# Token transposes ahead of the modulation with its columns tile by tile, and the last eight expert picks one by one, in a two-block transformer kernel on one core

## The chip, the core and the metric

The kernel is one program on one of the eight cores of a Trainium2 chip. TensorE (PE) multiplies matrices from SBUF into the eight banks of PSUM, VectorE (DVE) and ScalarE (ACT) do elementwise work, GpSimd (POOL) issues the indexed gathers, and SyncE's queue (SPq) issues the other transfers, which sixteen DMA engines carry out. The metric is the device time of one execution in microseconds (us).

## The reference

256 tokens of width 1024 pass two transformer blocks, all in float32. What the change touches is the first step of the first block and the last step of the second:

```python
# first block, the first step (c is one row of 1024; w_ada is 1024 x 6144)
mod = silu(c) @ w_ada + b_ada
shift1, scale1, gate1, shift2, scale2, gate2 = split(mod, 6)
hmix = rmsnorm(x, norm_mix_w) * (1.0 + scale1) + shift1
proj = hmix @ w_in                       # 1024 x 3600, all mixers' inputs
...
# second block, the last step (PEER): every token has 8 heads x 16 picks = 128 experts of 16384
act = gelu(einsum(u_tab[expert], x))     # one dot product of 1024 for each token and pick
w = gate * act
x = x + einsum(w, v_tab[expert])         # one row of 1024 for each token and pick
```

Between the two lie convolutions, a gated delta rule, window attention, a mixture of 32 experts, gated linear attention and block attention.

## The kernel before

Everything is written by engine: each of the five engines has its own list of instructions, and semaphores order them. Tokens are in two tiles of 128 (`t`), features in eight chunks of 128 (`k`).

**The head of the kernel.** The first block's matmuls are a hand-written list of jobs (`head_jobs`). A job has a name, a PSUM bank and the engine that empties it ("D" for DVE, "A" for ACT). TensorE fills the banks in that order and counts each job in the semaphore `hd`; before it writes a bank it waits until the last job of that bank has been emptied (`hbank`). DVE and ACT count what they empty in `ev_d` and `ev_a`. A job that is added by `add` takes the next bank of eight in turn.

SyncE loads c, x, the identity and ones, then four tiles of `w_ada` of 2 MB each (columns 0 to 2047: shift1 and scale1), a small tail of `w_in` (`in_tail`, 16 columns), and the first tiles of `w_in`, each 2 MB; the order is one queue.

DVE computes the root mean square of each token and writes the scaled tokens `h_tok` (L1927). TensorE multiplies the condition with each of the four tiles (`condition`, L1128): 8 matmuls with 512 columns, each of which the trace shows as two instructions, as for every float32 matmul here. DVE copies each result to `part1` (L1932). After the fourth copy the job `col` turns shift1 and scale1 into one column per chunk, by 16 matmuls with one column (L1140), and DVE makes `mod_t` of them (L1935 to L1938) and posts `mod1_ready`. TensorE has by then gone on to transpose the tokens (`xT0` to `xT3`, 16 transposes of 128 x 128, L1149). DVE (L1944) and ACT (L780) empty these four banks, and apply scale and shift of a chunk as they copy it from PSUM to `hT`, two chunks a bank, eight instructions with 256 columns in all. Then come the job `gab` (16 columns of `w_in`, L1120), and the projections `k0`, `k1`, `q0`, `q1`, `v0`, `v1` (L1114), each two chunks of 128 output features.

**The end of the kernel.** PEER's 256 picks (128 for each token tile) are gathered one by one: a pick brings one row of 2048 numbers for each of 128 tokens, u and v side by side, 1 MB. For pick `i` DVE takes the dot product (`dot`, L2726). In batches of `BATCH = 4`, ACT takes the GELU of four dot products (`applied`, L1056), DVE multiplies them by the gates (`weights`, L2734), and ACT makes four diagonal matrices of the products (L1063), in four buffers: diagonal `i` waits for `v_free` at `i - 3`. TensorE multiplies each diagonal with the v row in two halves (`values`, L1712) and accumulates in two banks over 128 picks. DVE issues its instructions in this order:

```python
for i in range(16 * N_STEP):
    if i >= 4:
        dot(i)
    if i >= 2 * BATCH and i % BATCH == 1:
        weights(i // BATCH - 1)
    ...
weights(16 * N_STEP // BATCH - 1)
result(1)
```

So the weights of picks 244 to 247 follow dot 249, those of 248 to 251 follow dot 253, and the last four follow dot 255. `result` adds the two finished banks to x (L2741) after the last pick, and SyncE writes each half out.

Of the kernel before, what the change touches and what calls it, by code (L numbers as in the profile page):

```python
# [15 lines left out]
ALU = mybir.AluOpType  # L16
ACT = mybir.ActivationFunctionType
# [98 lines left out]
def head_jobs():  # L116


    jobs = [("ada0", 0, "D"), ("ada1", 1, "D"), ("ada2", 0, "D"), ("ada3", 1, "D"), ("col", 2, "D"),
            ("xT0", 4, "D"), ("xT1", 5, "D"), ("xT2", 6, "A"), ("xT3", 7, "A"), ("gab", 3, "D")]  # L120
# [6 lines left out]
    for name in ("k0", "k1", "q0", "q1", "v0", "v1", "ss"):  # L127
        add(name, "D")
# [58 lines left out]
HEAD_OPS = {"col": 2, "xT0": 2, "xT1": 2, "xT2": 2, "xT3": 2, "k0": 4, "k1": 4, "q0": 4, "q1": 4, "v0": 4, "v1": 4,  # L187
# [117 lines left out]
UV_PLACES = 16  # L305
UV_PLAN = uv_plan(16 * TT * PH)
# [25 lines left out]
def two_blocks(nc, io):  # L332
    ctx = ExitStack()
    with ctx:
# [231 lines left out]
        h_ready = sem("h_ready")  # L566
        conv_scaled = sem("conv_scaled")
# [72 lines left out]
        diag_ready = sem("diag_ready")  # L640
        p_taken = sem("p_taken")
# [101 lines left out]
        def _(act):  # L743
# [30 lines left out]

            act.wait_ge(mod1_ready, 1)
            for g in (2, 3):
                b = halves(done(f"xT{g}"))
                for c in range(2):
                    k = 2 * g + c
                    act.activation(hT[:, k, :], b[:, c, :], ACT.Identity, scale=mod_t[:, 8 + k:9 + k],  # L780
                                   bias=mod_t[:, k:k + 1]).then_inc(ev_a, 1)
# [297 lines left out]
        def _(pe):  # L1079
# [52 lines left out]
            pe.wait_ge(cond_ready, 1)  # L1132
            for n in range(N_ADA1):
                b = hbank(f"ada{n}")
                hfull(condition(b, head_tile("ada", n)))
            b = hbank("col")
# [568 lines left out]
            def values(first, last_):  # L1705
                for i in range(first, last_):
# [144 lines left out]
        def _(dve):  # L1851
# [77 lines left out]

            for i in range(N_ADA1):  # L1930
# [17 lines left out]
            b = hjob("gab")  # L1948
            took(dve.tensor_copy(gab, b[:, 0:32].rearrange("p (a b) -> p a b", a=2)))
            hsync()  # L1950
            t3 = lambda ap: ap.rearrange("p (t c) -> p t c", t=TT)
            o(dve.tensor_tensor(t3(g_t), gab[:, :, 0:8], bc(dt_b.unsqueeze(1), [P, TT, 8]), ALU.add))
            post(gab_in)
# [18 lines left out]
            side_taps("k1", 6)  # L1972
            side_taps("q0", 0)
# [756 lines left out]
            def weights(b):  # L2730
                s, k = b * BATCH // 16, b * BATCH % 16
                sync()
                dve.wait_ge(gelu_done, b + 1)
                dve.tensor_tensor(w_cur[:, s, k:k + BATCH], gel[:, s, k:k + BATCH],  # L2734
                                  gates[:, s // 2, s % 2, k:k + BATCH], ALU.mult).then_inc(w_ready, 1)
# [41 lines left out]
            weights(16 * N_STEP // BATCH - 1)  # L2777
# [62 lines left out]
```

## Time and profile before

| | |
|---|---|
| median of three runs | 1695.36 us (1693.72 to 1697.14) |
| profiled execution, its own time | 1694.07 us |
| its span, first to last instruction | 1692.2 us |
| TensorE busy | 1475.6 us, 87% |
| VectorE busy | 784.0 us, 46% |
| ScalarE busy | 265.1 us, 16% |
| mean granted TensorE clock | 0.949 of full speed |
| data moved | 551.06 MB, mean 326 GB/s |

The span runs from the first to the last instruction; the execution's own time is 1.87 us more. Times in the rows are counted from the start of the span. The granted clock has two levels, shown as 1.00 (2.4 GHz) and 0.50 (1.2 GHz); a stretch that holds both shows a value between. The ends of matmuls are modelled, so the distance between starts is the safer measure of a matmul's price.

### The profile page before, as it was taken

The page shows a single profiled execution, that of the slowest core. Times are in us where ns is not written, and L with a number is a line of the kernel's source. Part 1 is how long each engine was busy: PE and PEld are TensorE (multiplying, and loading weights), DVE is VectorE, ACT ScalarE, POOL GpSimd, SP SyncE. Part 2 cuts the span into 40 slices and gives each one's busy share as a digit, 9 for nine tenths or more (in the row PEclk, how much of TensorE's full clock was granted, in tenths as well). Part 3 has the DMA queues.
Part 4 walks back from the last instruction along what each step waited for, and adds up shares of the span by engine and source line. Part 5 has one row for each costly group of instructions (what it writes and reads, how often), then busy time and mean ns, then how long its engine had stood idle before and what let it go on. Part 6 is the DMA issues. An engine that isn't in the chain of part 4 may idle for free.

```text
span 1692.2 us, 16785 instructions
## 1 busy us (share of the span) xinstructions
PE 1475.6 (87%) x6282; PEld 800.6 (47%) x6282; DVE 784.0 (46%) x1830; ACT 265.1 (16%) x644; POOL 308.1 (18%) x288
## 2 busy tenths in 40 slices
PE   4999999599999999999699798898777777787877
PEld 2897885444444444443446575553333333333333
DVE  2116754513232322322333466376766666676553
ACT  1312221100000000000033321222212121212111
POOL 0001000100000000000000012355444444444440
PEclk8999999699999999999899899999999999889999
DMA  9532347389999999999405138799999999999994
GB/s 376 226 108 96 147 150 298 130 344 427 428 428 427 426 423 427 427 429 428 203 33 216 51 137 304 305 376 422 421 422 421 421 422 421 422 421 421 421 422 200
DMA packets 60273, 551.06 MB, mean 326 GB/s; under 512 B 8608, under 2 KB 8896, under 8 KB 10400
## 3 DMA queue, kind: packets, MB, share of 16 engines
q1 hardware_dynamic: 22192, 277.47, 39.7%
q0 software_dynamic: 38000, 272.50, 39.4%
q8 instruction: 52, 0.85, 0.2%
q14 instruction: 29, 0.24, 0.0%
HBM read 548.90 MB, written 1.05 MB: 325 GB/s over the span
## 4 chain that ended last, share of the span: by engine, by line
PE 47%; DMA 39%; issue 5%; DVE 5%; POOL 2%; ACT 2%; SPq 0%; DVEq 0%; POOLq 0%; ACTq 0%
DMA ring<-peer_uv_d,work 19%; DMA ring<-expert_w_d 14%; PE ps L1462 9%; PE ps L1120 7%; PE ps L1712 7%; DMA consts_sb<-peer_uv_d,work 5%; PE ps L1212 5%; PE ps L1114 5%; PE ps L1571 4%; PE ps L1502 2%; PE ps L1451 1%; PE ps L1369 1%; DMA ring<-w_ada_d 1%; POOL ring L1845 1%; PE ps L1473 1%
## 5 line engine op out<-in xcount | busy, mean ns | idle before, releaser
L1712 PE MATMUL ps<-ring,work 128*128 128x512 f32 x752 | 364.6, 637 | 92.5 <-ACT work L1063 92.5
L2726 DVE CUSTOM_DVE_ANT_0 ring<-ring,work 128x1024 f32<-128x1024 f32 x188 | 229.8, 1223 | 134.8 <-DMA ring<-peer_uv_d,work 133.1
L1712 PEld LDWEIGHTS ps<-ring,work 128*128 128x128 f32 x752 | 149.3, 204 | 301.9 <-issue 178.9
L1845 POOL DMA_INDIRECT ring<-peer_uv_d,work x188 | 205.7, 1094 | 269.1 <-PE ps L1712 180.1
L1462 PE MATMUL ps<-ring,work 128*64 128x512 f32 x1024 | 226.6, 597 | 9.3 <-DMA ring<-expert_w_d 8.5
L1462 PEld LDWEIGHTS ps<-ring,work 128*64 128x64 f32 x1024 | 77.9, 138 | 154.8 <-issue 153.6
L1120 PE MATMUL ps<-ring,hT 128*128 128x512 f32 (+1 forms) x288 | 123.0, 586 | 1.7 <-issue 0.8
L1063 ACT ACTIVATE work<-consts_sb,work 128x128 f32<-128x128 f32 x256 | 82.3, 390 | 266.4 <-DVE work L2734 263.2
L1502 PE MATMUL ps<-ring,work 128*64 128x512 f32 x512 | 113.4, 595 | 0.7 <-DVE work L2356 0.7
L1712 PE MATMUL ps<-work 128*128 128x512 f32 x136 | 78.0, 703 | 39.9 <-ACT work L1063 39.9
L2352 DVE TENSOR_TENSOR work<-work,ps 128x512 f32<-128x512 f32 x16 | 11.0, 688 | 199.1 <-PE ps L1462 199.1
L1820 POOL DMA_DIRECT2D mod<-subkeys_d x1 | 0.5, 547 | 488.6 <-DVEq L2411 488.6
L1120 PEld LDWEIGHTS ps<-ring,hT 128*128 128x128 f32 x288 | 55.6, 196 | 63.1 <-issue 61.1
L1114 PE MATMUL ps<-hT,ring 128*128 128x256 f32 x352 | 79.6, 389 | 0.0
L922 ACT ACTIVATE work<-ps 128x512 f32<-128x512 f32 x16 | 9.6, 597 | 442.1 <-PE ps L1462 442.1
L1571 PE MATMUL ps<-hT,ring 128*128 128x128 f32 x640 | 73.8, 276 | 0.0
L1571 PEld LDWEIGHTS ps<-hT,ring 128*128 128x128 f32 x640 | 72.9, 193 | 1.5 <-issue 1.4
L1114 PEld LDWEIGHTS ps<-hT,ring 128*128 128x128 f32 x352 | 68.4, 196 | 9.6
L1212 PEld LDWEIGHTS ps<-ring 128*128 128x128 f32 x608 | 69.2, 192 | 5.2 <-issue 4.2
L1212 PE MATMUL ps<-ring 128*128 128x128 f32 x608 | 69.6, 275 | 0.8 <-ACT ring L853 0.8
L1451 PEld LDWEIGHTS ps<-work 128*128 128x128 f32 x512 | 60.0, 196 | 15.9 <-issue 12.2
L1502 PEld LDWEIGHTS ps<-ring,work 128*64 128x64 f32 x512 | 35.3, 137 | 67.4 <-issue 66.5
(388 smaller groups left out, 1502.3 us busy)
## 6 DMA issues: line engine op xcount, KB each, us to landing
ring<-expert_w_d SPq DMA_DIRECT2D x96, 2048.0 KB, 15.7
ring<-w_in_d SPq DMA_DIRECT2D x13, 2048.0 KB, 18.0
ring<-w_ada_d SPq DMA_DIRECT2D x12, 2048.0 KB, 8.1
ring<-w_out_d SPq DMA_DIRECT2D x4, 2048.0 KB, 8.0
ring<-peer_w_query_d SPq DMA_DIRECT2D x4, 2048.0 KB, 7.7
ring<-peer_uv_d,work POOLq DMA_INDIRECT x188, 23.4
mod<-b_ada_d SPq DMA_DIRECT2D x1, 2048.0 KB, 26.8
consts_sb<-consts_d SPq DMA_DIRECT2D x1, 1346.0 KB, 26.4
```

What stands on the lines that cost most here:

```text
L1063: act.activation(diag[:, k % 4, :], ident, ACT.Copy, scale=w_cur[:, s, k:k + 1]).then_inc(diag_ready, 1)
L1114: last = pe.matmul(b[0:n, at:at + T], wt[:, k, c0:c0 + n], hT[:, k, :], start=(k == 0), stop=(k == KC - 1))
L1120: last = pe.matmul(b[:, at:at + n], hT[:, k, t * P:(t + 1) * P], wt[:, k, c0:c0 + n], start=(k == 0), stop=(k == KC - 1))
L1212: last = pe.matmul(b[:, h * P:(h + 1) * P], lhsT(h), rhs(h), start=True, stop=True)
L1369: last = pe.matmul(ps[MID.bank(f"w{t}{n}")][:, :], mixT[k][:, t * P:(t + 1) * P], slot(N_HEAD - 2 + n)[:, k, :], start=(k == 0), stop=(k = ...
L1451: last = pe.matmul(b[:, c * P:(c + 1) * P], h_tok[:, t, k * P:(k + 1) * P], pm[:, t, :], start=(t == 0), stop=(t == TT - 1))
L1462: last = pe.matmul(b[u * CAP:(u + 1) * CAP, :], xeT[:, k, u * CAP:(u + 1) * CAP], wt[u][:, k, :], start=(k == 0), stop=(k == KC - 1), skip ...
L1502: last = pe.matmul(b[u * CAP:(u + 1) * CAP, :], actT[:, c, u * CAP:(u + 1) * CAP], wt[u][:, c, n * 512:(n + 1) * 512], start=(c == 0), sto ...
L1571: last = pe.matmul(b[0:n, at:at + P], wt[:, k, c0:c0 + n], hT[:, k, t * P:(t + 1) * P], start=(k == 0), stop=(k == KC - 1))
L1712: last = pe.matmul(ps[V_BANK[t] + n][:, :], diag[:, i % 4, :], v_row(i)[:, n * 512:(n + 1) * 512], start=(i % (16 * PH) == 0), stop=(i % ( ...
L1845: pool.indirect_dma_start(out=uv_rows(i), out_offset=None, in_=io["peer_uv"], in_offset=bass.IndirectOffsetOnAxis(ap=idx[:, s, k:k + 1], a ...
L2726: dve.tensor_tensor_reduce(out=u_row(i), in0=u_row(i), in1=h_tok[:, i // (16 * PH), :], scale=1.0, scalar=0.0, op0=ALU.mult, op1=ALU.add, ...
```

## The change

The four transposes' jobs move to the front of TensorE's list, before the first `w_ada` tile, and are emptied by plain copies (DVE two banks, ACT two banks). The columns of a `w_ada` tile are made right behind the matmuls of the next tile, so that only the fourth tile's columns (4 matmuls) are left when its copy is done. Eight matmuls of the identity with itself, whose result nothing reads (`warm`), follow each of the first three tiles. Scale and shift are then applied in place in `hT`: DVE takes chunks 0 to 4 and ACT chunks 5 to 7. The job `gab` moves behind `k1`, with its emptying on DVE behind that of `k1`, and takes a bank of the round, which moves the later jobs' banks by one. At the end, the last eight picks each get their own GELU, weights and diagonal; the weights of picks 244 to 247 follow dot 248 instead of dot 249; and the first half of the last result waits for the first half of the last pick alone (`half_done`).

```diff
-    jobs = [("ada0", 0, "D"), ("ada1", 1, "D"), ("ada2", 0, "D"), ("ada3", 1, "D"), ("col", 2, "D"),
-            ("xT0", 4, "D"), ("xT1", 5, "D"), ("xT2", 6, "A"), ("xT3", 7, "A"), ("gab", 3, "D")]
+    jobs = [("xT0", 4, "D"), ("xT1", 5, "D"), ("xT2", 6, "A"), ("xT3", 7, "A"), ("ada0", 0, "D"), ("ada1", 1, "D"),
+            ("ada2", 0, "D"), ("ada3", 1, "D"), ("col", 2, "D")]
...
-    for name in ("k0", "k1", "q0", "q1", "v0", "v1", "ss"):
+    for name in ("k0", "k1", "gab", "q0", "q1", "v0", "v1", "ss"):
...
+def batches(n):
+    return [(i, BATCH) for i in range(0, n - 8, BATCH)] + [(i, 1) for i in range(n - 8, n)]
+PICKS = batches(16 * TT * PH)
...
@@ ScalarE, head
+            for g in (2, 3):
+                act.activation(hT[:, 2 * g:2 * g + 2, :], halves(done(f"xT{g}")), ACT.Copy).then_inc(ev_a, 1)
             act.wait_ge(mod1_ready, 1)
-            for g in (2, 3):
-                b = halves(done(f"xT{g}"))
-                for c in range(2):
-                    k = 2 * g + c
-                    act.activation(hT[:, k, :], b[:, c, :], ACT.Identity, scale=mod_t[:, 8 + k:9 + k],
-                                   bias=mod_t[:, k:k + 1]).then_inc(ev_a, 1)
+            act.wait_ge(ev_a, head_evacuated("xT3"))
+            for k in (5, 6, 7):
+                act.activation(hT[:, k, :], hT[:, k, :], ACT.Identity, scale=mod_t[:, 8 + k:9 + k],
+                               bias=mod_t[:, k:k + 1]).then_inc(hx_a, 1)
@@ ScalarE, picks
-                for i in range(first, last, BATCH):
+                for b, (i, size) in enumerate(PICKS):
+                    if not first <= i < last:
+                        continue
                     s, k0 = i // 16, i % 16
-                    act.wait_ge(dotted, i + BATCH)
-                    act.activation(gel[:, s, k0:k0 + BATCH], dots[:, s, k0:k0 + BATCH], ACT.Gelu).then_inc(gelu_done, 1)
+                    act.wait_ge(dotted, i + size)
+                    act.activation(gel[:, s, k0:k0 + size], dots[:, s, k0:k0 + size], ACT.Gelu).then_inc(gelu_done, 1)
...
-                    act.wait_ge(w_ready, i // BATCH + 1)
-                    for k in range(k0, k0 + BATCH):
+                    act.wait_ge(w_ready, b + 1)
+                    for k in range(k0, k0 + size):
@@ TensorE, head
+            def warm(n):
+                for _ in range(n):
+                    pe.matmul(ps[3][:, 0:P], ident, ident, start=True, stop=True)
             pe.wait_ge(in_first, 16)
-            evacuated("ada3")
-            for c in range(4 * N_ADA1):
-                last = pe.matmul(b[:, c:c + 1], part1[:, c // 4, c % 4 * P:(c % 4 + 1) * P], ones[:, 0:1],
-                                 start=True, stop=True)
-            hfull(last)
             pe.wait_ge(h_ready, 1)
             for g in range(4):
                 b = hbank(f"xT{g}")
...
-            b = hbank("gab")
-            pe.wait_ge(in_tail, 16)
-            evacuated("xT1")
-            evacuated("xT3")
-            token_major(b, 0, 0, tail_w, 0, 16)
-            hfull(token_major(b, 16, 1, tail_w, 0, 16))
+            def columns(n):
+                b = ps[HEAD[HEAD_AT["col"]][1]]
+                evacuated(f"ada{n}")
+                for c in range(4 * n, 4 * n + 4):
+                    last = pe.matmul(b[:, c:c + 1], part1[:, n, c % 4 * P:(c % 4 + 1) * P], ones[:, 0:1],
+                                     start=True, stop=True)
+                return last
+            pe.wait_ge(cond_ready, 1)
+            for n in range(N_ADA1):
+                b = hbank(f"ada{n}")
+                hfull(condition(b, head_tile("ada", n)))
+                if n:
+                    columns(n - 1)
+                if n < N_ADA1 - 1:
+                    warm(8)
+            hbank("col")
+            hfull(columns(N_ADA1 - 1))
+            pe.wait_ge(hx_d, 5)
+            pe.wait_ge(hx_a, 3)
...
+                if name == "k":
+                    gate_columns()
@@ TensorE, picks
+                        if n == 0 and i == 16 * N_STEP - 1:
+                            last.then_inc(half_done, 1)
@@ VectorE, head
+            for g in range(2):
+                b = halves(hjob(f"xT{g}"))
+                took(dve.tensor_copy(hT[:, 2 * g:2 * g + 2, :], b))
             for i in range(N_ADA1):
...
-            for g in range(2):
-                b = halves(hjob(f"xT{g}"))
-                for c in range(2):
-                    k = 2 * g + c
-                    took(dve.tensor_scalar(hT[:, k, :], b[:, c, :], mod_t[:, 8 + k:9 + k], mod_t[:, k:k + 1],
-                                           ALU.mult, ALU.add))
+            dve.wait_ge(ev_a, head_evacuated("xT2"))
+            for k in range(5):
+                dve.tensor_scalar(hT[:, k, :], hT[:, k, :], mod_t[:, 8 + k:9 + k], mod_t[:, k:k + 1],
+                                  ALU.mult, ALU.add).then_inc(hx_d, 1)
...
             side_taps("k1", 6)
+            gates_in()
             side_taps("q0", 0)
@@ VectorE, picks
             def result(t):
                 for n2 in range(2):
-                    dve.wait_ge(v_free, 16 * PH * (t + 1))
+                    if t and n2 == 0:
+                        dve.wait_ge(half_done, 1)
+                    else:
+                        dve.wait_ge(v_free, 16 * PH * (t + 1))
...
-                if i >= 2 * BATCH and i % BATCH == 1:
+                if i >= 2 * BATCH and i % BATCH == 1 and i < 16 * N_STEP - 8:
                     weights(i // BATCH - 1)
+                if i == 16 * N_STEP - 8:
+                    weights((16 * N_STEP - 8) // BATCH - 1)
+                if i >= 16 * N_STEP - 8:
+                    weights((16 * N_STEP - 8) // BATCH + i - (16 * N_STEP - 8))
...
-            weights(16 * N_STEP // BATCH - 1)
             result(1)
```

## Rows read from the trace of the kernel before

**Rows 1.** The page's chain that ended last, shares of the span by engine.
```profile
PE 47%; DMA 39%; issue 5%; DVE 5%; POOL 2%; ACT 2%; SPq 0%; DVEq 0%; POOLq 0%; ACTq 0%
```

**Rows 2.** The chain in order of time, 0 to 110 us: start, us, what.
```profile
4.91 23.78 DMA ring<-w_ada_d
...
28.82 1.96 PE ps L1128 x16
...
30.80 0.70 DVE work L1932
...
31.64 4.88 PE ps L1140 x32
...
39.29 1.94 ACT hT L780 x4
...
41.36 4.43 PE ps L1120 x32
45.80 44.16 PE ps L1114 x192
```

**Rows 3.** Timeline, 0 to 45 us: start, us, engine, line, shapes, idle before.
```profile
6.16 19.21 SPq L687 DMA_DIRECT2D ring<-w_in_d x2
...
9.39 1.41 DVE L1927 TENSOR_SCALAR work<-x,small 128x1024 f32<-128x1024 f32 x2
...
13.85 3.39 PE L1128 MATMUL ps<-ring,work 128*32 128x512 f32 x16 [13.85 <-DMA ring<-w_ada_d]
...
23.64 3.62 PE L1128 MATMUL ps<-ring,work 128*32 128x512 f32 x16 [3.06 <-DMA ring<-w_ada_d]
...
36.38 3.65 PE L1149 MATMUL ps<-consts_sb,work 128*128 128x128 f32 x16
36.63 0.17 DVE L1935 TENSOR_TENSOR small<-ps,small 128x8 f32<-128x8 f32 x1 [5.14 <-PE ps L1140]
...
37.52 1.90 DVE L1944 TENSOR_SCALAR hT<-ps,small 128x256 f32<-128x256 f32 x4 [0.36 <-PE ps L1149]
```

**Rows 4.** Stretches of 2 us: busy time by engine (count), granted clock, DMA.
```profile
32.00:34.00 2.00, 2.00 (x19) 2.00 (x20) 0.00 (x0) 0.00 (x0) 0.00 (x0) 0.98 1.00 426
34.00:36.00 2.00, 2.00 (x12) 2.00 (x11) 0.00 (x0) 0.00 (x0) 0.00 (x0) 0.50 1.01 426
...
42.00:44.00 2.00, 2.00 (x20) 2.00 (x19) 0.00 (x0) 0.00 (x0) 0.00 (x0) 1.00 1.02 434
...
48.00:50.00 2.00, 2.00 (x6) 1.59 (x5) 0.00 (x0) 0.00 (x0) 0.00 (x0) 0.50 0.93 396
```

**Rows 5.** DMA issues from 6 to 15 us: KB, us to landing.
```profile
ring<-w_in_d SPq DMA_DIRECT2D x1, 2048.0 KB, 27.8
```

**Rows 6.** Groups by form, 30 to 250 us: busy us, mean ns.
```profile
L2048 DVE TENSOR_SCALAR work<-work,small 128x256 f32<-128x256 f32 x2 | 0.6, 342 | 0.0
```

**Rows 7.** Timeline of the end, from 1623 us.
```profile
1623.83 1.88 PE L1712 MATMUL ps<-consts_sb,work 128*128 128x512 f32 x4
1625.55 1.88 PE L1712 MATMUL ps<-work 128*128 128x512 f32 x4
...
1654.56 6.09 PE L1712 MATMUL ps<-ring,work 128*128 128x512 f32 x13
...
1658.48 1.23 DVE L2726 CUSTOM_DVE_ANT_0 ring<-ring,work 128x1024 f32<-128x1024 f32 x1 [1.26 <-DMA ring<-peer_uv_d,work]
...
1672.21 1.28 ACT L1063 ACTIVATE work<-consts_sb,work 128x128 f32<-128x128 f32 x4 [4.79 <-DVE work L2734]
...
1672.66 13.79 PE L1712 MATMUL ps<-ring,work 128*128 128x512 f32 x28 [2.77 <-ACT work L1063]
...
1675.80 1.23 DVE L2726 CUSTOM_DVE_ANT_0 mod<-mod,work 128x1024 f32<-128x1024 f32 x1 [1.23 <-DMA mod<-peer_uv_d,work]
...
1677.07 0.20 ACT L1056 ACTIVATE work<-work 128x4 f32<-128x4 f32 x1 [3.58 <-DVE work L2726]
...
1688.21 1.52 DVE L2741 TENSOR_TENSOR x<-x,ps 128x512 f32<-128x512 f32 x2 [10.67 <-PE ps L1712]
```

More of the change, by code:

```diff
@@ L184 @@
 HEAD_AT = {name: i for i, (name, _, _) in enumerate(HEAD)}
-HEAD_OPS = {"col": 2, "xT0": 2, "xT1": 2, "xT2": 2, "xT3": 2, "k0": 4, "k1": 4, "q0": 4, "q1": 4, "v0": 4, "v1": 4,
+HEAD_OPS = {"col": 2, "k0": 4, "k1": 4, "q0": 4, "q1": 4, "v0": 4, "v1": 4,
             "gc": 3, "kq0": 2, "kq1": 2, "kk0": 2, "kk1": 2}
@@ L566, in two_blocks @@
         h_ready = sem("h_ready")
+        hx_d = sem("hx_d")
+        hx_a = sem("hx_a")
         conv_scaled = sem("conv_scaled")
@@ L640, in two_blocks @@
         diag_ready = sem("diag_ready")
+        half_done = sem("half_done")
         p_taken = sem("p_taken")
@@ L1130, in condition @@
                 return last
[L1132 to L1136, printed above, removed]
-            pe.wait_ge(in_first, 16)
-            evacuated("ada3")
-            for c in range(4 * N_ADA1):
-                last = pe.matmul(b[:, c:c + 1], part1[:, c // 4, c % 4 * P:(c % 4 + 1) * P], ones[:, 0:1],
-                                 start=True, stop=True)
-            hfull(last)
+            def warm(n):
+                for _ in range(n):
+                    pe.matmul(ps[3][:, 0:P], ident, ident, start=True, stop=True)
+            pe.wait_ge(in_first, 16)
             pe.wait_ge(h_ready, 1)
@@ L1151, in _, with gate_columns @@
                 hfull(last)
-            b = hbank("gab")
-            pe.wait_ge(in_tail, 16)
-            evacuated("xT1")
-            evacuated("xT3")
-            token_major(b, 0, 0, tail_w, 0, 16)
-            hfull(token_major(b, 16, 1, tail_w, 0, 16))
+            def columns(n):
[17 more added lines that the diff above has]
+            pe.wait_ge(hx_a, 3)
+            def gate_columns():
+                b = hbank("gab")
+                pe.wait_ge(in_tail, 16)
+                token_major(b, 0, 0, tail_w, 0, 16)
+                hfull(token_major(b, 16, 1, tail_w, 0, 16))
             def two_chunks(name, wt, c0):
@@ L1939, in _, with gates_in @@
             post(mod1_ready)
-            for g in range(2):
-                b = halves(hjob(f"xT{g}"))
-                for c in range(2):
-                    k = 2 * g + c
-                    took(dve.tensor_scalar(hT[:, k, :], b[:, c, :], mod_t[:, 8 + k:9 + k], mod_t[:, k:k + 1],
-                                           ALU.mult, ALU.add))
-            dve.wait_ge(in_small, 80)
-            b = hjob("gab")
-            took(dve.tensor_copy(gab, b[:, 0:32].rearrange("p (a b) -> p a b", a=2)))
-            hsync()
+            dve.wait_ge(ev_a, head_evacuated("xT2"))
+            for k in range(5):
+                dve.tensor_scalar(hT[:, k, :], hT[:, k, :], mod_t[:, 8 + k:9 + k], mod_t[:, k:k + 1],
+                                  ALU.mult, ALU.add).then_inc(hx_d, 1)
+            dve.wait_ge(in_small, 80)
+            def gates_in():
+                b = hjob("gab")
+                took(dve.tensor_copy(gab, b[:, 0:32].rearrange("p (a b) -> p a b", a=2)))
+                hsync()
+                o(dve.tensor_tensor(t3(g_t), gab[:, :, 0:8], bc(dt_b.unsqueeze(1), [P, TT, 8]), ALU.add))
+                post(gab_in)
             t3 = lambda ap: ap.rearrange("p (t c) -> p t c", t=TT)
-            o(dve.tensor_tensor(t3(g_t), gab[:, :, 0:8], bc(dt_b.unsqueeze(1), [P, TT, 8]), ALU.add))
-            post(gab_in)
             scaled = [0]
@@ L2730, in weights @@
             def weights(b):
-                s, k = b * BATCH // 16, b * BATCH % 16
+                i, size = PICKS[b]
+                s, k = i // 16, i % 16
                 sync()
                 dve.wait_ge(gelu_done, b + 1)
-                dve.tensor_tensor(w_cur[:, s, k:k + BATCH], gel[:, s, k:k + BATCH],
-                                  gates[:, s // 2, s % 2, k:k + BATCH], ALU.mult).then_inc(w_ready, 1)
+                dve.tensor_tensor(w_cur[:, s, k:k + size], gel[:, s, k:k + size],
+                                  gates[:, s // 2, s % 2, k:k + size], ALU.mult).then_inc(w_ready, 1)
             def result(t):
                 for n2 in range(2):
-                    dve.wait_ge(v_free, 16 * PH * (t + 1))
+                    if t and n2 == 0:
+                        dve.wait_ge(half_done, 1)
+                    else:
+                        dve.wait_ge(v_free, 16 * PH * (t + 1))
                     xs = x[:, t, n2 * 512:(n2 + 1) * 512]
```

## The prediction

> **What bounds the kernel now.** I read the chain that ended last first, as shares: TensorE and DMA hold 86% of it between them [rows 1], so a gain exists only where the change shortens what one of these two waits for. Then the same chain in order of time over the head [rows 2]. The reader is to see three stretches there. Up to 28.7 us the chain is the loading of the four `w_ada` tiles. From 28.8 to 45.8 us it is a relay, with no transfer in it: fourth tile's matmuls, its copy, 32 column instructions (L1140), transposes, scale and shift (ACT, L780), `gab` (L1120). From 45.80 us it is 44.16 us of unbroken projections, to 89.96 us. The relay is what the head's part of the change attacks. The timeline [rows 3] says what TensorE does before: it works 3.39 us on the first tile at 13.85 us and then waits for tiles, while the scaled tokens, which the transposes need, are finished at 9.39 + 1.41 = 10.80 us.
>
> The stretches of 2 us [rows 4] show the granted clock. TensorE is busy all the time from 31.64 us, yet the level falls from 1.00 to 0.50 at 34 us, and it is at 0.50 again at 48 to 50 us, in `k0`. So the relay is partly run at 1.2 GHz: 19 one-column instructions in 2 us at the high level, 12 at the low one.
>
> For the end I read the timeline [rows 7]. Dot 248 starts at 1658.48 and dot 255 at 1675.80 us: 17.32 / 7 = 2.47 us from dot to dot, each released by its gather. TensorE needs less for a pick: 1625.55 - 1623.83 = 1.72 us for four matmul instructions. It idles between batches, and at the end the idle time turns against it: the diagonals of picks 248 to 251 are made only at 1672.21 us, behind dot 253, and from 1672.66 us TensorE has eight picks before it, until the result's add starts at 1688.21 us, 11.1 us after the last dot. The eight picks take 15.5 us instead of 8 x 1.72 + 0.2 = 13.9: the first of them run at the lower level, after 2.77 us of idling.
>
> **The head, step by step.** Removed from the relay: the transposes, 28 - 4 = 24 of 32 column instructions (12 of 16 matmuls), and `gab`, which is not saved but moved between `k1` and `q0`.
>
> *Transposes first.* They can start at about 10.9 us and cost 3.65 us as in [rows 3], at the low level, so they end at 14.6 us. The first tile's matmuls start at 14.6 instead of 13.85 us. Its cover: the second tile is the next event and lands some 4.9 us after the first (23.78 us of loading hold four tiles and 1 MB of x before them [rows 2]). The plain copies (two by DVE, two by ACT) fall in time in which both engines wait. They cost nothing; without that cover a DVE copy of a bank costs 0.70 us [rows 2].
>
> *Per tile.* At the high level: 1.96 us for the tile [rows 2], 8 x 0.105 = 0.84 us for the earlier tile's columns (19 in 2 us [rows 4]), and the eight extra matmuls, 16 instructions at 3.65 / 16 / 2 = 0.114 us, so 1.83 us. The sum is 4.6 us, under the 4.9 us between tiles, with 0.3 us to spare: nothing at the high level. At the low level: 3.62 + 8 x 0.167 + 3.65 = 8.6 us, and TensorE would fall behind the transfers. I take the high level, because the engine would be busy over 90% of the time from 11 us on, where before it had gaps of 3 us ahead of the tiles that ran low [rows 3].
>
> *From the fourth tile to the projections.* The copy ends at 31.50 as before [rows 2]; columns start at 31.64. Only 8 instructions are left: 0.84 us, to 32.5 (bound from above 8 x 0.167 = 1.3 us). DVE needed from 36.52 (end of columns) to 37.52 - 0.36 = 37.16 us for `mod_t` [rows 2, 3], 0.64 us, so 33.1. Then DVE scales five chunks and ACT three. ACT: 3 x 1.94 / 4 = 1.45 us [rows 2]. DVE reads from SBUF now, which the trace shows for one instruction form with one scalar pointer: 0.3 us each [rows 6]; from PSUM it took 1.90 / 4 = 0.475 us [rows 3]. Bounds 1.5 and 2.4 us; I take 1.5, since the SBUF row is the same operation and width. The chunks are ready at 34.65, the first `k0` matmul starts at 34.8 us. Its weights are not late: the tile was issued at 6.16 [rows 3] and landed 27.8 us later [rows 5], at 33.96 us, and the queue's order is unchanged. The margin is 0.8 us. The transfers behind it are needed 7 us or more after they land.
>
> The Trainium skill (VectorE: DVE Perf Modes, "The perf-mode tier table") gives float32 scaling from SBUF twice the rate of the same from PSUM. The two rows agree in direction, 0.3 against 0.475 us; by the page the sum stays, and by the PSUM row alone the forecast would be 0.9 us later.
>
> *Projections.* 45.63 to 89.96 us is 44.3 us for six banks, its slow start included. With `gab` inside: 3.2 us at the high level (20 instructions in 2 us [rows 4]) or 4.43 us as measured [rows 2]; I take 3.8, between. So `v1` ends at 34.8 + 44.3 + 3.8 = 82.9 instead of 89.96 us: **7.0 us earlier**. Behind `gab` only `q0` waits on TensorE. DVE's copy of `gab` and ACT's gate functions come later, but `q0` occupies TensorE for 7 us in the meantime; if that cover failed the loss would be some 2 us for DVE and ACT, which is itself hidden until `ss`.
>
> The unsure term is the clock. The low level cost `k0` about 44.2 - 192 x 0.2175 = 2.4 us here (13.92 us for the 64 instructions that follow at the high level, from the same chain). If the level is high at 34.8 us, the gain is 9.4; if it falls once more behind `gab`, whose 16-column matmuls are as thin as the columns at which it fell at 34 us, it is 5.3.
>
> The Trainium skill (TensorE: Matmul & The Clock Gate, "What's actually happening") says that the throttled state is the default and activity releases it; by that rule the extra matmuls would carry the high level through to `k0`, and the sum would be 2.4 us less. The trace does not agree fully: the level fell at 34 us in a TensorE that was busy throughout, with one-column matmuls [rows 4]. I go by the row.
>
> All that follows the projections is passed on in time: TensorE stays the bound, and the expert weights and gathers start when earlier stages free them. The banks shifted by one wait for jobs at least seven places back, as before.
>
> **The end, step by step.** Weights of 244 to 247 now follow dot 248, which ends at 1658.48 + 1.23 = 1659.7. With 0.2 us for the weights and 0.4 for the first diagonal, pick 244 is ready at 1660.4 us, and TensorE is busy with 240 to 243 until 1660.6 [rows 7]. From there it need not stop: 12 picks x 1.72 + 0.2 = 20.8, so the last pick ends at 1681.2 us if each diagonal is there in time. It is: a single pick costs 1.23 + 0.1 us dot, 0.1 + 0.20 GELU, 0.1 + 0.15 weights, 0.4 diagonal: DVE is held 2.0 us of the 2.47 us between landings. The new wait is in DVE's order: dot i+1 stands behind the GELU of pick i, that behind diagonal i-1 on ACT, and that behind pick i-5 on TensorE. For dot 249 this means 1661.6 instead of 1660.96; for later ones pick i-5 is long done. Dot 255 ends at 1677.0, its diagonal is there by 1678.0, and TensorE reaches that pick at 1679.5: TensorE is the bound, by 1.5 us. Against 1688.2 that is 7.0 us. The low level at the batch start goes too, as there is no idle time before it (it is in the 7.0; a fall at an earlier batch would cost 1.7 back).
>
> *Half result.* The first add (half of 1.52 = 0.76 us) runs beside the last half pick; the second add and its store follow the last matmul: 0.8 us less. The end: **7.8 us**.
>
> **Sum.** 7.0 + 7.8 = 14.8 us. The profiled execution took 1694.07 us (span 1692.2 + 1.87), so 1679.3. It lies 1.3 us under the median of the runs, so the forecast is 1680.6 us.
>
> **Rivals.**
>
> A. *TensorE falls behind in the `w_ada` stage*, because the extra matmuls run at the low level. For: the first tile did (3.39 us) and the third (3.62 us) [rows 3]. Against: it was idle before each. Then 14.6 + 4 x 3.6 + 3 x (1.3 + 3.65) - 1.3 = 42.5 for the fourth tile, `k0` at 46.6, `v1` at 94.7: 4.7 us later than before, in all 1695.4 + 4.7 - 7.8 = 1692.3 us.
>
> B. *The single picks do not keep TensorE fed.* Should the round trip exceed 2.47 us, dots fall behind their landings. The 7.0 us are gone when the last dot is 7.0 + 1.5 us late, so at 8.5 / 8 = 1.1 us a pick too much, 3.5 us in all. Then only the head's gain remains: 1688.4 us. For: three engines hand over eight times. Against: the 0.5 us to spare.
>
> C. *The head's gain is given back later*, by a stage bound by transfers that do not move: 1687.6 us. Against: the projections run unbroken [rows 2], and each later transfer waits for a buffer.
>
> D. *The high level lasts through `k0`*, carried by the extra matmuls: 2.4 us less, 1678.2 us. Against: the columns and the scaling leave TensorE with thin work and then none from 30.8 to 34.8 us, longer than the stretch in which it fell [rows 4]. This is what the clock page's rule would make of it.
>
> E. *Slower.* The single picks run one after another, TensorE included, because each waits for the one before through a shared buffer or order. At the high level 2.0 + 0.4 + 1.7 = 4.1 us a pick, at the low level, which such gaps bring, 5.8. Eight from 1658.5 end at 1704.9 us, 16.7 later than now; less the head's 7.0 and 0.8: 1704.3 us. It decides from 4.6 us a pick. Against: four diagonal buffers.
>
> **How the numbers follow.** Forecast 0.60, A 0.07, B 0.09, C 0.03, D 0.18, E 0.03. The forecast's own spread: level fallen again behind `gab` 1.7 worse, PSUM price 0.9, `gab` 0.6 either way, tail clock 1.7, and 1.7 us between runs: 1678 to 1686; with D and the runs' spread below it, and B's and C's values above, the range is 1675.5 to 1688.5. Within 0.2% (3.4 us, about what a measurement of this kernel can tell from no change) lies A alone, half of it a little faster. Faster 0.91, same 0.06, slower 0.03.
>
> **What would show it.** Right: transposes at 11 us; TensorE waiting for each tile by name of the transfer; first `k0` matmul at 34 to 36 us; the stretch from it to `ss` about 48 us; no idle time in TensorE from pick 244 on; 4.5 us from last dot to last matmul. Wrong: a tile's matmuls starting later than its landing, a dot that waits for ACT instead of its gather, or a granted clock of 0.50 between 15 and 31 us.

## The result and the profile after

| | before | changed |
|---|---|---|
| median | 1695.12 us | 1680.2 us |
| profiled execution, its own time | 1694.07 us | 1681.18 us |
| its span | 1692.2 us | 1679.4 us |

The ratio of the changed kernel to the one before is 0.9914, 95% interval [0.9892, 0.9936]: 14.6 us faster (10.8 to 18.3). The forecast was 1680.6 us and 14.8 us. Beside the experiments the changed kernel was timed again: 0.9910 [0.9893, 0.9927]. The two profiled executions lie 12.9 us apart by their own times, 12.8 us by their spans.

The chain of the changed kernel in order of time, from 0 to 110 us, answers to [rows 2]:

```profile
4.96 24.97 DMA ring<-w_ada_d
...
30.07 1.92 PE ps L1142 x16
31.99 1.89 PE ps L1165 x16
...
34.65 1.72 DVE hT L1978 x5
...
36.41 15.48 PE ps L1128 x64
51.89 3.48 PE ps L1134 x32
55.37 29.41 PE ps L1128 x128
84.78 4.42 PE ps L1203 x32
```

The relay between the last tile and `k0` has shrunk to columns (L1165) and scaling (L1978), 4.4 us from 31.99 to 36.41; before it was 15.0 us, from 30.78 to 45.80 [rows 2]. `gab` (L1134) stands between `k1` and `q0`. `v1` ends at 84.78 instead of 89.96 us: 5.2 us, where 7.0 were forecast. The matmuls of the fourth tile start at 30.07 us and not at 28.82, because the tile landed later, although no edit touches its transfer; the experiments `e3_nowarm` and `e5_wide` look into that.

The timeline of the same stretch, against [rows 3]:

```profile
11.70 3.65 PE L1157 MATMUL ps<-consts_sb,work 128*128 128x128 f32 x16 [11.70 <-DVEq L1899]
...
15.28 1.95 PE L1142 MATMUL ps<-ring,work 128*32 128x512 f32 x16
...
17.15 2.05 PE L1148 MATMUL ps<-consts_sb 128*128 128x128 f32 x16
...
23.86 1.92 PE L1142 MATMUL ps<-ring,work 128*32 128x512 f32 x16
...
30.07 1.92 PE L1142 MATMUL ps<-ring,work 128*32 128x512 f32 x16 [1.40 <-DMA ring<-w_ada_d]
...
34.65 1.71 DVE L1978 TENSOR_SCALAR hT<-hT,small 128x256 f32<-128x256 f32 x5
```

All four tiles run at the high level (1.92 to 1.95 us), where the first and third took 3.4 and 3.6. The second and the third tile start without a wait, so TensorE reaches them a little after they have landed; the fourth waits 1.40 us for its transfer. Five scalings take 1.71 us, 0.34 each.

The stretches of 2 us, against [rows 4] (the column behind the busy times is the granted clock):

```profile
34.00:36.00 2.00, 0.00 (x0) 0.00 (x0) 1.73 (x8) 1.41 (x3) 0.00 (x0) 0.97 1.00 426
36.00:38.00 2.00, 1.59 (x4) 1.32 (x5) 0.36 (x2) 0.18 (x1) 0.00 (x0) 0.50 0.90 366
...
56.00:58.00 2.00, 2.00 (x7) 1.65 (x6) 0.00 (x0) 1.95 (x5) 0.25 (x1) 0.59 0.97 414
58.00:60.00 2.00, 2.00 (x6) 1.56 (x6) 0.00 (x0) 1.97 (x3) 0.00 (x0) 0.56 0.99 416
```

The level falls twice here: behind the gap ahead of `k0`, as forecast, and behind `gab`, which the prediction held for possible at 1.7 us. The 128 instructions of `q0` to `v1` take 29.41 us here and 27.72 us in every experiment with the new head below: 1.7 us.

The end, against [rows 7]:

```profile
1655.30 1.98 PE L1743 MATMUL ps<-work 128*128 128x512 f32 x4 [0.35 <-ACT work L1077]
...
1656.39 1.23 DVE L2763 CUSTOM_DVE_ANT_0 ring<-ring,work 128x1024 f32<-128x1024 f32 x1
...
1660.55 13.90 PE L1743 MATMUL ps<-ring,work 128*128 128x512 f32 x32
...
1670.79 1.22 DVE L2763 CUSTOM_DVE_ANT_0 mod<-mod,work 128x1024 f32<-128x1024 f32 x1 [0.73 <-DMA mod<-peer_uv_d,work]
...
1672.06 0.20 ACT L1070 ACTIVATE work<-work 128x1 f32<-128x1 f32 x1 [1.56 <-DVE work L2763]
...
1675.34 0.69 DVE L2782 TENSOR_TENSOR x<-x,ps 128x512 f32<-128x512 f32 x1 [2.82 <-PE ps L1743]
...
1676.20 0.69 DVE L2782 TENSOR_TENSOR x<-x,ps 128x512 f32<-128x512 f32 x1 [0.17 <-PE ps L1743]
```

and the chain has it as one piece:

```profile
1655.30 20.88 PE ps L1743 x48
```

Twelve picks without a gap in 20.88 us (20.8 were forecast), behind 0.35 us of waiting for the first diagonal. (The 13.90 us row is a part of the same piece: the view breaks it where the tiles change.) From the last dot product's start to the last matmul's end it is 1676.18 - 1670.79 = 5.39 us, forecast 5.4, before 1688.18 - 1675.80 = 12.38. Dot 249 waits for ACT as forecast (1656.39 us, behind the GELU of pick 248), and the ones after it wait for their gathers. From the last matmul to the end of the span: 3.22 us, before 4.02.

### The profile page after: what moved, and what is told of

Its sections match the earlier page's. It is cut to its first block, busy times and chain, and to the rows that moved or that the text cites. A ratio compares the mean times of both kernels' runs of the same rounds, so it can differ in the third digit from the quotient of the medians.

```text
span 1679.4 us, 16908 instructions
## 1 busy us (share of the span) xinstructions
PE 1476.9 (88%) x6330; PEld 805.8 (48%) x6330; DVE 786.1 (47%) x1839; ACT 267.3 (16%) x651; POOL 307.2 (18%) x288
## 4 chain that ended last, share of the span: by engine, by line
PE 46%; DMA 40%; issue 5%; DVE 4%; POOL 2%; ACT 2%; SPq 1%; DVEq 0%; POOLq 0%
DMA ring<-expert_w_d 17%; DMA ring<-peer_uv_d,work 16%; PE ps L1493 8%; PE ps L1134 8%; PE ps L1743 7%; DMA consts_sb<-peer_uv_d,work 5%; PE ps L1128 5%; PE ps L1243 5%; PE ps L1602 4%; DMA ring<-w_ada_d 1%; PE ps L1400 1%; POOL ring L1878 1%; PE ps L1533 1%; PE ps L1482 1%; PE ps L1142 1%
## 5 line engine op out<-in xcount | busy, mean ns | idle before, releaser
L1134 PE MATMUL ps<-ring,hT 128*128 128x512 f32 (+1 forms) x288 | 122.1, 582 | 1.7 <-ACT hT L948 0.8
L1134 PEld LDWEIGHTS ps<-ring,hT 128*128 128x128 f32 x288 | 55.2, 194 | 62.5 <-issue 60.4
```

The source lines that it names most:

```text
L1134: last = pe.matmul(b[:, at:at + n], hT[:, k, t * P:(t + 1) * P], wt[:, k, c0:c0 + n], start=(k == 0), stop=(k == KC - 1))
```

## The experiments

| kernel | median us | ratio to before | `k0` starts | `v1` ends | last dot to last matmul |
|---|---|---|---|---|---|
| before | 1695.12 | 1 | 45.80 | 89.96 | 12.4 |
| changed | 1680.2 | 0.9914 [0.9892, 0.9936] | 36.41 | 84.78 | 5.4 |
| changed, again (e11_control) | 1678.53 | 0.9910 [0.9893, 0.9927] | 36.48 | 84.11 | 5.4 |
| e1_head | 1685.26 | 0.9950 [0.9935, 0.9965] | 36.49 | 84.35 | 10.9 |
| e2_tail | 1688.78 | 0.9958 [0.9943, 0.9974] | 48.26 | 91.21 | 5.4 |
| e3_nowarm | 1684.03 | 0.9933 [0.9915, 0.9951] | 35.63 | 83.17 | 7.7 |
| e4_fill | 1683.76 | 0.9934 [0.9917, 0.9950] | 38.64 | 83.66 | 7.4 |
| e5_wide | 1678.51 | 0.9913 [0.9897, 0.9929] | 35.10 | 82.84 | 7.7 |
| e6_shift | 1688.15 | 0.9960 [0.9945, 0.9974] | 36.37 | 83.34 | 9.4 |
| e7_warm24 | 1688.9 | 0.9965 [0.9952, 0.9978] | 44.61 | 91.57 | 7.4 |
| e8_gabsplit | 1678.26 | 0.9912 [0.9899, 0.9925] | 36.60 | 83.57 | 5.4 |
| e9_last12 | 1677.49 | 0.9897 [0.9881, 0.9913] | 36.68 | 83.53 | 4.2 |
| e10_all | 1676.55 | 0.9888 [0.9870, 0.9905] | 35.55 | 80.81 | 4.2 |
| e12_nohalf, a single run | 1678.86 | | 36.28 | 83.75 | 6.5 |

Each ratio is to runs of the kernel before beside that experiment, whose medians lie between 1694.6 and 1695.1 us. The last three columns are one profiled execution each, read from the chain. A kernel's runs spread over 1.2 to 12 us, so steps of 1 to 2 us are read from the traces, and the ratios decide only between larger ones.

**The head's part alone** (`e1_head`: the changed kernel with the end as before):

```diff
-    return [(i, BATCH) for i in range(0, n - 8, BATCH)] + [(i, 1) for i in range(n - 8, n)]
+    return [(i, BATCH) for i in range(0, n, BATCH)]
...
+            weights(16 * N_STEP // BATCH - 1)
             result(1)
```

> The head's part alone: the end is as in the kernel before. If the two parts add up, the first k0 matmul starts at 34.8 to 36.5 us, the projections with gab take 48 us, v1 ends 5 to 7 us earlier than in the kernel before, and the end is unchanged: 11 to 12.4 us from the end of the last dot product to the start of the last adds. Time 5 to 7 us under the kernel before, ratio 0.996 to 0.997. Rival: later stages give the head's gain back, then the last dot product is at 1675.8 us as before and the ratio is 1.000.

The ratio gives 8.5 us (5.9 to 11.0), more than the 5 to 7 expected. `v1` ends 5.6 us earlier. The end's chain:

```profile
1663.03 14.02 PE ps L1743 x32
```

Here the last eight picks take 14.0 us, against 15.5 before [rows 7]: the level did not fall on the last batch, so the end is 10.9 us and not 12.4. Those 1.5 us of the old end depend on where a low stretch falls. The last dot product starts at 1666.15 us, 9.7 us earlier than before and 4.0 us more than `v1` gained: the give-back rival is out, and the stages between the two differ from trace to trace.

**The end's part alone** (`e2_tail`: the kernel before with the edits of picks, weights and half result):

> The end's part alone. If TensorE is kept busy by the single picks, 48 matmul instructions run without a gap, the last dot product to the last matmul is 5.4 us instead of 12.4, and the last store ends 3.2 us behind the last matmul instead of 4.0: 7.8 us under the kernel before where the low clock fell on the last batch, 6.1 where it did not; ratio 0.9954 to 0.9964. Rival: the end profits only because the head shifted the gathers, then under 3 us.

The ratio gives 7.1 us (4.4 to 9.7), inside the first theory and above the rival's 3. The chain has the same single piece as the changed kernel, with no edit in the head:

```profile
41.28 6.98 PE ps L1130 x32
...
1663.62 20.88 PE ps L1722 x48
```

The first line is `gab` in the old head: the granted clock is 0.50 throughout it, and it takes 6.98 us where the trace of the kernel before had 4.43 [rows 2]; `v1` ends at 91.21 us. The old head varies by at least 1.25 us from execution to execution, and against this one the new head of `e1_head` is 6.9 us earlier.

The product of the two ratios, 0.9950 x 0.9958 = 0.9908, is the changed kernel's 0.9910 to 0.9914: within the intervals the parts add up.

**Without the extra matmuls** (`e3_nowarm`):

```diff
-                if n < N_ADA1 - 1:
-                    warm(8)
```

> The changed kernel without its 24 extra identity matmuls. Theory: they keep the granted clock high but buy little, because each tile's matmuls and columns fit between two tiles even at the low level (3.6 + 1.3 us of 4.9): only what stands behind the fourth tile can lose, its own matmuls 1.7 us and eight columns 0.5 us, so the same time to 2.2 us slower, with stretches of 0.50 between 17 and 31 us. Rival: without them the level is low through the columns and all of k0 as well, 4 to 6 us slower.

The chain over the head:

```profile
6.27 29.12 DMA ring<-w_in_d
...
35.63 16.34 PE ps L1128 x64
```

Stretches of 0.50 appear at about 23 to 27 us and from 33 us, much as before the change, yet the fourth tile's matmuls start at 28.73 us and `v1` ends at 83.17 us, 0.9 us before the control. By the trace the extra matmuls bring nothing; the ratios, 0.9933 against 0.9910, overlap and do not settle it. The rival (4 to 6 us slower) is out for the trace. Two things were not expected: the fourth tile is back at its old time, and the first `w_in` tile is now what `k0` waits for: it landed at 35.4 us, where the prediction had 33.96 [rows 3, 5].

**The gap filled** (`e4_fill`):

```diff
+            warm(20)
             pe.wait_ge(hx_d, 5)
```

> The changed kernel with 20 more identity matmuls behind the last columns, where TensorE has no work for 2.5 us. They take 4.6 us at the high level if all are issued, so k0 starts about 2 us later than its chunks are ready. Theory: the level falls in k0 because TensorE has thin or no work from 32 to 36.4 us; with the gap filled the low stretch at 36 to 38.6 us is gone (1.3 us less), while the overlap costs 2 us: same to 1 us slower, and the trace shows 1.00 from 34 to 50 us. Rival: the level falls whatever stands in the gap, then the stretch is still there and the kernel is 2 us slower.

```profile
34.07 4.57 PE ps L1148 x40
38.64 13.81 PE ps L1128 x64
```

`k0` starts 2.2 us later than in the control, but `k0` and `k1` take 13.8 us, the high level throughout, against 16.4 us there: `v1` ends 0.45 us earlier. With the gap ahead of `k0` filled the low stretch is gone, as the theory had it. It costs 1.7 us in the changed kernel's trace and 2.6 in the control's. The ratio, 0.9934, does not tell the two kernels apart.

**Fewer and wider extra matmuls** (`e5_wide`):

```diff
-                    warm(8)
+                    warm_wide(2)
...
+            def warm_wide(n):
+                for _ in range(n):
+                    pe.matmul(ps[3][:, :], ident, h_tok[:, 0, 0:512], start=True, stop=True)
```

> The changed kernel with its eight narrow extra matmuls per tile (16 multiply and 16 load instructions) replaced by two wide ones, the identity with 512 columns of the scaled tokens (4 and 4 instructions), the same 1.7 to 1.8 us of TensorE. In the traces of the three kernels with the narrow ones the fourth tile's matmuls start at 30.1 to 30.3 us, in those without at 28.7 to 28.8, and only the former show a packet of instruction loading between 27 and 28.5 us. Theory: TensorE's longer instruction list is what delays the tile; then it starts at 28.7 us here with the level still at 1.00, and the packet comes after 28.5 us and delays the first w_in tile instead (k0 at 35.3 to 35.7). Rival: the busier TensorE itself slows the transfer; then the fourth tile still starts at 30 us. Time: within 2 us of the changed kernel either way.

```profile
28.76 1.92 PE L1142 MATMUL ps<-ring,work 128*32 128x512 f32 x16 [0.24 <-DMA ring<-w_ada_d]
```

The tile is back at 28.76 us with TensorE as busy as in the changed kernel and the level at 1.00, so the rival is out: it is not TensorE's work that slows the transfer. In the list of DMA queues from 27 to 28.5 us the changed kernel has, beside the data's queue, one line that this one lacks:

```profile
q8 instruction: 1, 0.02, 4.2%
```

Over all traces it goes together: eight traces with the narrow extra matmuls have such a packet (16 KB) between 24 and 28.5 us and start the fourth tile at 29.9 to 30.3 us; in five it is absent there (before, e2, e3, e5, e10), and the tile starts at 28.7 to 28.9. In `e7_warm24` it comes at 22 to 24.4 us, and TensorE is too late there to show when the fourth tile landed. The first `w_in` tile, next in the queue, says the same. This is the changed kernel's, issued at 6.45 us, so landed at 35.05 us:

```profile
ring<-w_in_d SPq DMA_DIRECT2D x1, 2048.0 KB, 28.6
```

It landed at 33.9 to 34.0 us in the three traces whose packet comes after 33 us (before, e2, e5), and at 35.0 to 35.5 us in the eleven whose packet comes earlier, e3 and e10 with a packet at 30 to 33 us among them. By the row above, 4.2% of 16 engines over 1.5 us, the packet occupies one of the sixteen engines for about 1.0 us (an estimate). That the packet makes what is in the queue some 1.3 us later is a correlation over 14 traces and one experiment that moved it; which engine's instructions it carries, the profile does not say, and the cause stays open to that extent. The second half of the expectation (the packet right behind 28.5 us) did not come true: it came after 36 us, and nothing waited. The ratio, 0.9913 against the control's 0.9910, shows no gain.

**Order alone at the end** (`e6_shift`: head's part, batches of four to the end, their weights one dot earlier):

```diff
+                if i in (16 * N_STEP - 8, 16 * N_STEP - 4):
+                    weights(i // BATCH - 1)
```

> The head's part and, of the end's part, only the order: the weights of picks 244 to 247 behind dot 248 and those of 248 to 251 behind dot 252, still four at a time, no half result. If the end's 7.0 us come from TensorE never waiting, this keeps a wait of 2.9 us between the two batches: from the last dot product's start to the last matmul 12.4 - 2.4 = 8.3 to 10.0 us (the upper one with a low clock behind the wait), against 5.4 with single picks and 10.9 in the head-only kernel. Rival: the order alone is enough, then it is near 6 us and the single picks buy nothing.

```profile
1670.25 7.15 PE ps L1743 x16
```

9.4 us from last dot to last matmul, of 10.9 in the head-only kernel: the order alone gives 1.5 us in the trace, within the expected 8.3 to 10.0. The ratios, 0.9960 against 0.9950, do not show it. The piece shows why: the last batch of four starts behind its own last dot, so that four picks (7.15 us) stand behind it; with single picks TensorE has 4.2 us left behind the end of the last dot, the time of little more than two.

**Many more extra matmuls** (`e7_warm24`: `warm(24)` for `warm(8)`):

> The changed kernel with 24 extra matmuls per tile instead of 8: 5.6 us of TensorE, with the tile's own 1.9 and columns 0.9 8.4 us against 4.9 us from tile to tile. Rival A of the prediction at the high level: TensorE falls behind the transfers, the fourth tile's matmuls start at about 14.7 + 3 x 8.4 - 0.9 = 39 us instead of 30, and the kernel is 9 us slower than the changed one, so about 6 us faster than the kernel before. If the head's time were set by something else than TensorE's own order, it would stay where it is.

```profile
32.87 5.47 PE ps L1148 x48
38.33 1.85 PE ps L1142 x16
...
42.85 1.72 DVE hT L1978 x5
```

Rival A's mechanism, made real: TensorE is late, the fourth tile starts at 38.3 us (expected 39), `k0` at 44.6, and the time is 1688.9, 5.7 us under the kernel before (expected about 6). So TensorE's own work sets the pace of this stage once it is longer than the time from tile to tile, here 8.3 us a tile against about 4.9. How close to 4.9 us the limit lies was not tested.

**`gab` in two pieces** (`e8_gabsplit`: one token tile behind `k0`, one behind `k1`):

```diff
+                    if name == "k":
+                        b = ps[HEAD[HEAD_AT["gab"]][1]]
+                        pe.wait_ge(in_tail, 16)
+                        last = token_major(b, 16 * c, c, tail_w, 0, 16)
```

> The changed kernel with the two token tiles of gab apart, one behind k0 and one behind k1, 1.8 us of thin matmuls each instead of 3.5 us in one piece. Theory: the level falls behind gab because of the thin matmuls in one stretch (the changed kernel's trace has 0.5 at 56.4 to 59.8 us, the head-only one and two others have none, so it is a matter of where it falls): here no stretch of 0.50 between 45 and 70 us, up to 1.7 us less than the trace with one and no change against those without. Rival: k0's low stretch behind it is what counts, the split changes nothing.

No low stretch from 42 to 70 us, and `v1` at 83.57 us. But the control's trace and eight others with `gab` in one piece have none either. Only the changed kernel's first trace has it. The expectation is met and tells little: inconclusive.

**Twelve single picks** (`e9_last12`: 12 for 8 in the list of batches and in DVE's order):

> The changed kernel with the last twelve picks single instead of eight. In the traces of four kernels TensorE starts picks 240 to 243 at the low level (start to last matmul 30.3 to 30.7 us for 64 instructions, 27.4 at the high level), and the last matmul then ends 7.4 to 7.7 us behind the last dot product's start; in the others it ends 5.4 behind it. Theory: in both cases TensorE, not the gathers, sets the end, so an earlier start at pick 240 (2.5 us) gives 1 to 2.5 us: the last dot to the last matmul is 4.1 to 5.4 us. Rival: the chain of single picks is the limit, then it stays at 5.4 or grows.

```profile
1670.00 0.41 ACT work L1077
1670.45 2.00 PE ps L1743 x4
1672.47 0.69 DVE x L2782
```

4.2 us from last dot to last matmul: TensorE now waits for each of the last picks, so it is no longer what sets the end. The trace gives 1.2 us; the intervals of the ratios, 0.9897 against 0.9910, overlap.

**All together** (`e10_all`: e5, two wide matmuls in the gap, e8 and e9):

> All that the runs point to: wide extra matmuls (2 per tile), two more of them behind the last columns, where TensorE has nothing to do for 2.5 us, gab in two pieces, and twelve single picks. Theory: the fourth tile's matmuls start at 28.8 us, the first k0 matmul at 35.1 to 35.5, the level stays 1.00 from 15 to 84 us, v1 ends at 80.2 to 80.8 us (84.8 in the changed kernel), and the end gains 1 to 2.5: 4 to 6 us less than the changed kernel's control run. Rival: the level falls in k0 all the same, as the two wide matmuls leave 0.7 us idle: then v1 ends 1.7 to 3.4 us later than that.

```profile
35.55 7.14 PE ps L1128 x32
...
80.81 3.73 PE ps L1208 x32
```

The level stays at 1.00 from 15 us through `v1`, which ends at 80.81 us, 3.3 us before the control; the end is 4.2 us. In `e5_wide`, which lacks the two wide matmuls in the gap and the split of `gab`, `v1` ends at 82.84 us, 2.0 us later. The median is 1676.55 us, the lowest of all kernels here, its ratio 0.9888 [0.9870, 0.9905]. That is 18.4 us under the kernel before by the medians; the step over the control (2 us by the medians, 4 to 6 expected) is less than the intervals can tell.

**The control** (`e11_control`, the changed kernel again):

> The changed kernel itself once more, beside the others on the same chip: 14 to 15 us under the kernel before by either theory; its trace shows how far the stretches vary from one execution to the next, above all whether the fourth tile starts at 30 us again (theory: yes, since the instruction list is the same) or at 28.8 us.

The fourth tile starts at 30.14 us again. Another part differs. The chain behind `v1` is, in the changed kernel's first trace,

```profile
84.78 4.42 PE ps L1203 x32
89.20 16.30 PE ps L1128 x64
```

and in the control's

```profile
84.11 3.47 PE ps L1203 x32
87.58 13.92 PE ps L1128 x64
```

The first line is `ss` with its one-column matmuls, the second the projections behind it. From `v1`'s end to the first output projection (273.1 us before, 271.3 in the changed kernel's first trace) it is 183.1, 184.9 or 186.5 us in all 14 traces, and the whole difference lies in these two pieces: none, one or two low stretches of 1.7 us. The changed kernel's first trace had two and was unlucky; the control's, with none, is 4.0 us earlier at the first output projection, and its span is 1675.5 us instead of 1679.4.

**Without the half result** (`e12_nohalf`):

```diff
-                        if n == 0 and i == 16 * N_STEP - 1:
-                            last.then_inc(half_done, 1)
```

> The changed kernel without the half result: both last adds wait for the last matmul. From the last matmul to the end of the span 4.0 us instead of 3.2 us, the 0.8 us of the prediction's last term. Rival: the store's own time is the limit and nothing changes.

```profile
1643.58 29.45 PE ps L1743 x64
1673.04 0.70 DVE x L2777
```

From the last matmul (1673.03 us) to the end of the span (1677.1 us) it is 4.1 us, as in the kernel before: the half result is worth 0.8 us in the traces.

## Why the prediction was right, step by step

*The whole.* Forecast 1680.6 us, measured 1680.2 and 1678.5. The head's 7.0 and the end's 7.8 us were measured alone as 8.5 (5.9 to 11.0) and 7.1 (4.4 to 9.7), and they add up. That the median was met to 0.4 us is luck: the interval is nearly 4 us to either side, and the profiled execution gained 12.9 us where the sum gave 14.8. The missing 1.9 us are nearly all the head's, in the terms below.

*Transposes first, at no cost.* Right in the main: they run from 11.70 us (10.9 forecast), and the second tile's matmuls start at 19.13 us where they started at 18.65 us before. TensorE catches up by the fourth tile, so nothing is lost.

*Per tile 4.6 of 4.9 us.* Right: 23.86 - 19.13 = 4.73 us from the second tile to the third, with no wait, and e7 shows what happens well beyond the budget. In the control TensorE waits 0.41 and 0.20 us for these two tiles, in the changed kernel's trace not at all: the margin was nearly used up. That the extra matmuls were needed for it was not claimed, and e3 shows that they are not. Rival A did not occur.

*Fourth tile to `k0`: 34.8 us forecast, 36.41 measured, outside the 34 to 36 us that the prediction named as its sign.* This is the term that was mis-sized. The relay itself was forecast at 4.0 us from the end of the tile's matmuls and took 4.4. Five scalings took 1.71 instead of 1.5 us; the row that the prediction used has 342 ns each [rows 6], five of which are 1.71, but it was read as 0.3. The other 1.25 us stand ahead of it: the tile landed later, which the prediction excluded with "the queue's order is unchanged". The order is; e5 shows that the extra matmuls' form decides it. The first `w_in` tile was to land 0.8 us before `k0` and landed at 35.05 us, behind the start that was forecast: even with a faster relay `k0` would have had to wait for it, as it does in e3.

The Trainium skill (VectorE: DVE Perf Modes, "The perf-mode tier table") gives float32 scaling from SBUF twice the rate of the same from PSUM. The traces agree in direction only: 0.34 us from SBUF against 0.475 us from PSUM, a factor of 1.4.

*Projections with `gab` 48.1 us.* Measured 48.4 in the changed kernel, 47.6 in the control. Its parts were off against each other: `gab` 3.5 instead of 3.8, the low level in `k0` 1.7 instead of 2.4 us, and once more 1.7 behind `gab`. With such a fall behind `gab` the prediction gave the head 5.3 us, and 5.2 were measured; that these agree is chance, since the late tile was not in it.

*Rival D, the high level through `k0`.* It did not occur: TensorE has no matmul for 2.54 us ahead of `k0`, and the level is 0.50 from 36 us. It falls there with the extra matmuls and without them (e3), and stays up when the gap itself is filled (e4, e10).

The Trainium skill (TensorE: Matmul & The Clock Gate, "What's actually happening") has the throttled state as the default and activity as what releases it. The prediction read from it that extra matmuls between the tiles would carry the level through `k0`, which the trace does not show; that filling the gap keeps it up agrees with the page.

*The rest is passed on in time.* Nothing is given back: the head alone gives at least 5.9 us by its ratio. Whether exactly what `v1` gained arrives is not shown. From `v1`'s end to the last dot product single traces differ by 6 us (1581.8 to 1587.9), the kernel before with 1585.8 among them.

*The end 7.0 + 0.8 us.* Right to 0.1 us in the trace, for the reason given: TensorE never waits once it has begun pick 244 (e6, where it does, loses 4 us). Part of it is luck as well: 1.5 of the 7.0 us are a low stretch that the trace of the kernel before had in its last batch and e1 had not. Rivals B and E did not occur. The prediction named a dot that waits for ACT as a sign of being wrong, while its own sum had dot 249 do so; it did, and it cost nothing. In five of the traces with eight single picks (e3, e4, e5, e7, e12) TensorE has 64 instructions ahead of it from pick 240 on, with a low stretch at their start in each, and the last matmul ends 6.5 to 7.7 us behind the last dot, 1.1 to 2.3 us more than forecast. The prediction had a fall at an earlier batch at 1.7 us. With twelve single picks (e9, e10) it is 4.2 us.

## What to carry to other kernels

Where the chain runs as a relay between engines, ask of each link whether it needs what came before: here the transposes, three quarters of the columns and `gab` did not, and moving them made `v1` end 5 to 7 us earlier in the traces (5.9 to 11.0 us of the time by the ratio) without making any of them faster. How much each of the three moves gives alone was not tested. At an end that is fed by transfers, count what is left to do behind the last arrival, and make the batches small enough there that the engine behind them neither waits nor has more than a pick or two left. Extra matmuls between the tiles bought nothing here; those in the gap directly ahead of the dense work kept the clock up (e4, e10), and wide ones take fewer instructions for the same time. What they give, 2 us at most in the traces, is less than the ratios can tell.

## What the hardware showed unexpectedly

A 16 KB packet of the instruction queue in the stream of weight tiles goes with tiles that land 1.1 to 1.6 us later; that it is the cause is not fully shown. The granted clock also fell while TensorE was busy without a break: at 34 us before the change, behind one-column matmuls [rows 4], and in some executions in or behind `ss` (one column) and `gab` (16 columns). Each such low stretch cost about 1.7 us; where they fall differs from execution to execution of the same kernel, and moved one span against another by nearly 4 us.
